# A mixture-of-experts trunk layer: fewer filler matmuls at the start, some in the last pair's waits, and a tail scattered by halves

## The reference

```
h_lat = modulate(rmsnorm(x, g_mix), mod[0], mod[1])     # and h_ctx from ctx
y_lat = token_mixer(h_lat, h_ctx, w_in, ...)
x = x + mod[2] * y_lat
f = modulate(rmsnorm(x, g_ffn), mod[3], mod[4])
# 16 experts in 4 groups; each token goes to the best 2 of its best group
for e in range(16):
    he = silu(f @ w_gate[e]) * (f @ w_up[e])
    y = y + combine[:, e:e + 1] * (he @ w_down[e])
x = x + mod[5] * y
return rmsnorm(x, g_final)
```

## Time and profile before

| | us |
|---|---|
| three runs | 739.55, 743.22, 737.66 |
| median | 739.55 |
| profiled execution, its own time | 739.38 |
| its span, first to last instruction | 737.6 |
| TensorE matmul busy | 704.3 (95% of the span) |
| mean granted TensorE clock | 0.986 |

### The profile page before, as it was taken

One profiled execution on the slowest core, in us unless ns is written; L12 is line 12 of the kernel. 1 busy time (PEld: TensorE's weight loads), 2 busy tenths in 40 slices (PEclk: granted clock), 3 DMA queues, 4 the chain that ended last, 5 costly groups with the idle time before them and its releaser, 6 DMA issues.

```text
span 737.6 us, 7936 instructions
## 1 busy us (share of the span) xinstructions
PE 704.3 (95%) x3260; PEld 419.1 (57%) x3260; DVE 286.8 (39%) x492; ACT 112.3 (15%) x197; POOL 165.9 (22%) x119
## 2 busy tenths in 40 slices
PE   9999999999999999999999999998999999998875
PEld 5334586555775467776877788556434443443321
DVE  2558262877220475644243323235302221220224
ACT  4012011111001322221212320012000000000012
POOL 0137679789197000700000000000000000000020
PEclk9999999999999999999999999998999999999988
DMA  8965355651441333323553235982999999999992
GB/s 357 421 269 202 125 223 198 251 199 58 171 171 58 114 115 120 130 93 115 221 235 113 71 131 207 423 334 120 392 418 423 422 421 423 423 421 423 423 417 96
DMA packets 26388, 183.39 MB, mean 249 GB/s; under 512 B 2928, under 2 KB 3312, under 8 KB 10608
## 3 DMA queue, kind: packets, MB, share of 16 engines
q1 hardware_dynamic: 24336, 176.36, 60.0%
q10 hardware_dynamic: 1440, 4.42, 1.5%
q0 software_dynamic: 576, 2.10, 0.7%
HBM read 178.14 MB, written 4.72 MB: 248 GB/s over the span
## 4 chain that ended last, share of the span: by engine, by line
PE 83%; SPq 7%; DMA 4%; DVE 3%; issue 1%; ACT 0%; DVEq 0%
PE bank L731 17%; PE bank L1096 15%; PE bank L735 9%; PE bank L727 7%; SPq L363 7%; PE bank L748 6%; DMA sb<-expert_w 4%; PE bank L754 4%; PE bank L953 3%; PE bank L1071 3%; PE bank L878 2%; PE bank L899 2%; PE bank L780 2%; PE bank L886 2%; PE bank L741 2%
## 5 line engine op out<-in xcount | busy, mean ns | idle before, releaser
L1096 PE MATMUL bank<-sb 128*64 128x512 f32 x768 | 173.2, 608 | 10.0 <-DMA sb<-expert_w 8.9
L731 PE MATMUL bank<-sb 128*128 128x256 f32 x576 | 128.5, 381 | 0.6 <-PE bank L727 0.3
L1096 PEld LDWEIGHTS bank<-sb 128*64 128x64 f32 x768 | 57.0, 140 | 119.5 <-issue 118.5
L731 PEld LDWEIGHTS bank<-sb 128*128 128x128 f32 x576 | 108.1, 190 | 17.8 <-issue 3.8
L525 POOL DMA_INDIRECT sb<-y_rows,slot_rows x4 | 3.9, 979 | 391.6 <-DMA y_rows<-sb 390.7
L485 POOL TENSOR_TENSOR sb<-sb 128x1024 f32<-128x1024 f32 x32 | 66.4, 2076 | 60.2 <-DMA sb<-ada_w 58.0
L735 PE MATMUL bank<-sb 128*128 128x512 f32 x160 | 70.2, 593 | 0.3 <-PE bank L731 0.3
L1282 DVE COPY sb<-bank 128x512 f32<-128x512 f32 x45 | 29.2, 685 | 105.4 <-PE bank L886 67.2
L727 PE MATMUL bank<-sb 128*128 128x512 f32 x128 | 55.8, 593 | 0.3 <-PE bank L953 0.3
L735 PEld LDWEIGHTS bank<-sb 128*128 128x128 f32 x160 | 29.8, 190 | 35.3 <-issue 35.3
L1613 DVE TENSOR_TENSOR sb<-sb,bank 128x512 f32<-128x512 f32 x8 | 5.5, 689 | 110.8 <-PE bank L1096 110.8
(11 more groups left out here) (237 smaller groups left out, 661.3 us busy)
## 6 DMA issues: line engine op xcount, KB each, us to landing
sb<-expert_w SPq DMA_DIRECT2D x96, 1024.0 KB, 22.1
sb<-front_w SPq DMA_DIRECT2D x19, 2048.0 KB, 8.1
sb<-ada_w SPq DMA_DIRECT2D x32, 512.0 KB, 3.6
sb<-ada_mix SPq DMA_DIRECT2D x4, 2048.0 KB, 19.5
y_rows<-sb ACTq DMA_DIRECT2D x7, 512.0 KB, 7.8
sb<-xcT SPq DMA_DIRECT2D x4, 512.0 KB, 6.3
sb<-front_w SPq DMA_DIRECT2D x4, 512.0 KB, 20.2
sb<-na_bias SPq DMA_DIRECT2D x1, 1536.0 KB, 12.5
```

Source lines behind the costliest of these rows:

```text
L731: ins = pe.matmul(ps[:, c * L:(c + 1) * L], lhs(w, k, (2 * i + c) * P), hT[:, k, 0:L], start=(k == 0), stop=(k == KD - 1))
L1096: ins = pe.matmul(bank[e * CAP:(e + 1) * CAP, :], lhsT[:, k, e * CAP:(e + 1) * CAP], slot[pair_[e]][:, o + k * 512:o + (k + 1) * 512], sta ...
```

## The change

Five edits, in the order of the diff:

- `WARM[0]` goes from 12 to 7: five matmuls of zeros fewer ahead of the row sums.
- `stay_warm(n)` runs n matmuls of 128x512 on constants into bank 1, which nobody reads. One stands ahead of each half of the last pair's `up` (in `two_experts`, for `m == 3 * LAST + 1`), two stand ahead of the first half of its `down`. All stand before the wait for the weights.
- For the last pair TensorE scatters each half directly after its half of `down`: down 0, scatter 0, down 1, scatter 1.
- DVE's order becomes: three of the four gathered blocks, `experts_out` of half 0, the fourth block, `scattered` of half 0, `scaled_tokens`, `experts_out` of half 1, `scattered` of half 1.
- The two loops at the end become one: reciprocal and scaling of token block 0, then of block 1.

```diff
--- before.py
+++ after.py
@@ -81,7 +81,7 @@
 FILLS = [f for g in FRONT if g[:3] != "out" for f in group_fills(g)]
 FILLS += [(f"out{i}", t, "dve") for t in range(NT) for i in range(2)]
 PBANKS = 3
-WARM = (12, 4, 1, 3)
+WARM = (7, 4, 1, 3)
 BANK_OF = [7 if f[:2] == ("ff", 3) else n % PBANKS for n, f in enumerate(FILLS)]
 ROW_GROUPS = (4, 5, 10, 11)
 POOLED = (6, 7, 8, 9, 4, 5, 10, 11)
@@ -1085,10 +1085,17 @@
                 for s in RING[r]:
                     pe.wait_ge(w_in_[s], slot_value(s) + 16 * (5 - LAST) + n * 16)
 
+            def stay_warm(n):
+
+                for _ in range(n):
+                    pe.matmul(banks[1][:, :], ident, small[:, 0:512], start=True, stop=True)
+
             def two_experts(bank, pair_, parts, lhsT, o=0, m=None, n=None):
 
                 for k in range(parts):
                     if m is not None and k % 4 == 0:
+                        if m == 3 * LAST + 1:
+                            stay_warm(1)
                         take_half(m, k // 4)
                     if n is not None and k % 4 == 0:
                         pe.wait_ge(h_out, 2 * n + (k // 4 + 1))
@@ -1134,10 +1141,10 @@
                     ins = pe.transpose(banks[7][:, t * P:(t + 1) * P], SW_now[:, t, :], ident)
                 ins.then_inc(turn_ready, 1)
 
-            def scatter(n):
+            def scatter(n, halves=range(2)):
 
                 pe.wait_ge(cutT_ready, n - (LAST - 1))
-                for i in range(2):
+                for i in halves:
                     pe.wait_ge(y_out, 2 * n + (i + 1))
                     for t in range(NT):
                         pe.matmul(banks[(0, 1, 7, 2)[2 * i + t]][:, :], ST_now[:, t, :], y_sb[:, i * 512:(i + 1) * 512],
@@ -1155,9 +1162,12 @@
                 if n < LAST:
                     gather(n + 1, S_now[(n + 1) % 2], (1,))
                 for i in range(2):
+                    if n == LAST and i == 0:
+                        stay_warm(2)
                     take_half(3 * n + 2, i)
                     down(n, RING[(3 * n + 2) % 5], (i,))
-            scatter(LAST)
+                    if n == LAST:
+                        scatter(n, (i,))
             n_pass = pe.value_load(passes[0:1, 0:1], min_val=1, max_val=MAXPASS)
             with pe.If(n_pass > 1):
                 with pe.Fori(1, n_pass) as p:
@@ -1622,26 +1632,26 @@
                 for t in range(NT):
                     ins = dve.tensor_tensor(xg[:, t, :], x_nat[:, t, 0:512], g_last[:, 0:512], ALU.mult)
 
-            def scattered(n):
-                for i in range(2):
+            def scattered(n, halves=range(2)):
+                for i in halves:
                     for t in range(NT):
                         dve.wait_ge(scat_ready, 4 * (n - LAST) + (2 * i + t + 1))
                         y = x_nat[:, t, 512 * i:512 * i + 512]
                         ins = dve.tensor_tensor(y, y, banks[(0, 1, 7, 2)[2 * i + t]][:, :], ALU.add)
                         ins.then_inc(scat_out, 1)
 
-            def experts_out(n):
+            def experts_out(n, halves=range(2)):
 
                 if isinstance(n, int):
                     dve.wait_ge(y_stored, 16 * n)
-                for i in range(2):
+                for i in halves:
                     dve.wait_ge(down_ready, 2 * n + (i + 1))
                     cols = slice(512 * i, 512 * i + 512)
                     dve.tensor_tensor(y_sb[:, cols], banks[4 + i][:, :], row5[:, cols], ALU.mult).then_inc(y_out, 1)
 
-            def gathered_back():
-
-                for q in range(2 * NT):
+            def gathered_back(rows):
+
+                for q in rows:
                     dve.wait_ge(y_in[q], 16)
                     if q >= NT:
                         dve.drain()
@@ -1671,12 +1681,15 @@
             n_pass = dve.value_load(passes[0:1, 0:1], min_val=1, max_val=MAXPASS)
             gated(LAST)
             turned_out(LAST)
-            gathered_back()
-            experts_out(LAST)
-            scattered(LAST)
+            gathered_back(range(2 * NT - 1))
+            experts_out(LAST, (0,))
+            gathered_back((2 * NT - 1,))
+            scattered(LAST, (0,))
             dve.wait_ge(glast_in, 16)
             dve.wait_ge(scat_out, NT)
             scaled_tokens()
+            experts_out(LAST, (1,))
+            scattered(LAST, (1,))
             with dve.If(n_pass > 1):
                 with dve.Fori(1, n_pass) as p:
                     dve.drain()
@@ -1701,7 +1714,6 @@
             for t in range(NT):
                 dve.wait_ge(fin_root, t + 1)
                 dve.reciprocal(stat[:, 2 + t:3 + t], stat[:, 2 + t:3 + t]).then_inc(fin_rec, 1)
-            for t in range(NT):
                 dve.wait_ge(fin_rec, t + 1)
                 dve.scalar_tensor_tensor(out=normed[:, t, 512:1024], in0=x_nat[:, t, 512:1024], scalar=stat[:, 2 + t:3 + t],
                                          in1=g_last[:, 512:1024], op0=ALU.mult, op1=ALU.mult).then_inc(fin_by["dve"], 1)
```

## The result

| | us |
|---|---|
| kernel before, median of 6 (lowest, highest) | 739.15 (737.66, 743.22) |
| changed kernel, median of 6 (lowest, highest) | 733.27 (732.99, 734.46) |
| ratio | 0.9907, 95% interval 0.988 to 0.9934 |
| profiled execution: own time, span | 733.21, 731.4 |

The ratio stands as recorded; the quotient of the two medians is 0.992. The changed kernel is faster by 0.93%, just under 1%; 735.6 had been forecast, 0.53%. The measured time lies inside the range, but the gain is larger than the sum by more than the measurement leaves open. In the two profiled executions it is 739.38 - 733.21 = 6.17 us, against a sum of 3.97.

The account below looks back on a forecast made before the run. TensorE was taken as the bound, its start passing through the weight stream to the end. 739.38 - 2.15 - 0.92 - 0.9 = 735.4 us for the profiled execution, 0.17 below its median, so 735.6; range 732.5 to 739.0.

Parts of the forecast that it names:

- The bound: Whole kernel: TensorE frees the weight stream's slots, so a microsecond saved at the start moves the stream's end by one.
- The start is hidden: Rival at the start: second gain fails and a modulation block holds TensorE back; 737.4 us, chance 0.13.
- Part 1, five fillers: Start, ahead of the row sums: five fewer warm-up matmuls, at full clock, gain 2.15 us; lower bound 1.2.
- the 0.4 of slack: Start: row sums end at 13.9, so ACT's preparation of the root, ending at 13.52, is in time by 0.4 us.
- The slow rival: Rival at the start: a gap keeps the row sums at half clock, 5.0 us lost; 743.7 us, chance 0.07.
- Part 1, the second gain: First projection: four modulations finish before GpSimd's first big multiply, removing TensorE's wait; gain 0.92 us, bounds 0 and 0.92.
- Part 2, fillers in the last pair: Last pair's up and down waits: fillers keep the clock up; down half 0 takes 3.65 instead of 5.35 us.
- no effect at the end: Last pair: fillers alone are worth nothing, since down's last half waits for weights landing at 722.3 and already takes 3.65.
- Part 3, the tail: From down's last half to the end: scatter by halves and merged final loops gain 0.9 us; bounds 0.3 and 1.3.
- the new wait: Tail: half 0's scatter delays down's last half by 0.36 us; then DVE, not TensorE, starts the last experts_out at 726.8.
- the last wait eats the tail: Rival in the tail: third gathered block lands 2 us later, delaying down's last half; 737.5 us, chance 0.14.
- The clock at the routing: Rival at 504.5 to 511.3 us: the half-clock stretch falls less low, 3.4 us gained; 732.2 us, chance 0.12.

Follow-up runs that it names:

- e1: Kernel before with seven instead of twelve matmuls of zeros at the start, nothing else of the change; median 736.44 us, ratio 0.994.
- e7: Kernel before with twenty-four instead of twelve matmuls of zeros at the start; median 744.0 us, ratio 1.0057.
- e4: Kernel before with one added wait: GpSimd's first big multiply waits until VectorE has modulated all eight blocks; median 739.46 us, ratio 0.997.
- e9: Kernel before, unchanged, run again for a second profile; median 738.98 us.
- e2: Changed kernel with twelve instead of seven matmuls of zeros at the start again; median 736.75 us, ratio 0.9968.
- e10: Kernel before, unchanged, run again for a third profile; median 743.07 us.
- e6: Changed kernel with three instead of seven matmuls of zeros at the start; median 736.13 us.
- e3: Changed kernel without the four filler matmuls in the last pair (both stay_warm calls removed); median 736.2 us, ratio 0.9947.
- e5: Kernel before with the four filler matmuls in the last pair's waits and nothing else; median 741.47 us, ratio 1.0026.
- e8: Changed kernel with six instead of four filler matmuls on TensorE while VectorE works out the routing; median 731.94 us, ratio 0.9899.
- e12: Changed kernel with six routing fillers, the four final stores reordered and the last issued by ScalarE; median 731.21 us, ratio 0.9886.
- e11: Kernel before with fourteen instead of twelve matmuls of zeros at the start; median 741.76 us.

## Why the prediction was right and wrong

**The bound.** Right. The start passes to the end through the weight stream in full: -3.08 at 56 us and -3.08 at 719 (e1), +4.52 and +4.57 (e7). "The start is hidden" is refuted. In single profiles the middle and the routing can hide it (e4, e9).

**Part 1, five fillers.** Forecast 2.15; measured 1.89 (e1) and 2.62 (after). The step from 2.15 to either is the time at which the clock rises, which differs by execution: behind twelve fillers the sums start at 9.03 in before, at 8.59 in e2 and at 9.65 in e10. Also, ScalarE takes over as the limit at 13.5 us, as the 0.4 of slack had it, so fewer fillers than seven bring no more (e6, 13.32). `ada_mix` held nothing up. The slow rival does not occur: even three fillers leave the sums at full clock.

**Part 1, the second gain.** The mechanism was right and the place too; the size was not. This is the step that failed for the kernel's times: "gain 0.92. The bounds are 0 and 0.92". I took one profile's outcome of a race as the largest there is. In that profile it was 1.18 (root to p1 43.30 against 42.12; I left out a second, shorter break in the x16), and in the one profiled execution of the upper group, which holds over a third of them, it is 4.4 with what the clock adds. A price that depends on 0.07 us between two starts, 48.75 and 48.82 (48.77 and 48.88 in e9, where it is nothing), had to be bounded by the worse order, and the first sign was in the table: three runs at 737.66, 739.55 and 743.22. I read these as noise of 1.5 us, where they were two groups.

**Part 2, fillers in the last pair.** Right in what they do to half 0 of `down` (3.65), and in that they can gain only with part 3. Their worth there is 1.4 (e3), close to the delay of 1.3 that I had ahead of the last half; the distance between my bounds was 0.6 all the same (0.9 against 0.3), since I let VectorE's queue hide 0.7 of that delay. It hid nothing: from the last half to the end e3 takes 13.62, as after. What I had as "no effect at the end" by themselves is a loss of 1.7 (e5). The trace of before could not tell me: that its last half ran in 3.65 hung on a wait of 1.22, and I did not ask what a faster half 0 makes of that wait.

**Part 3, the tail.** Forecast 0.9, measured 1.53 (e2, e3, after, to 0.01). Two terms were mis-sized. The first is the drain behind the gathered blocks: I took the 0.52 of idle ahead of L1640 for it, and it stands at two places of my sum. After, the next operation starts 0.07 behind a gathered block (718.71 to 718.78). What the 0.52 was stays open. Without it the scatter of half 0 is done by 717.81, and the 0.36 of delay that I had for the last half shrinks to under 0.1; VectorE is free at 721.46, when TensorE ends its half at 721.45, so the new wait never comes about. The addition ends 7.28 behind the start of the last half instead of 8.01: 0.73 against my 0.33. The second is the stretch from there to the end, 6.33 instead of 7.14: 0.80 against 0.57. The rival "the last wait eats the tail" did not occur in after, where the third gathered block was done at 713.88, 1.0 ahead of half 0 of `down` (714.91). In small it did occur: in e2, e6, e8 and e12 that block was done 0.2 to 0.4 behind half 0, and the last half started up to 0.3 later against its weights than in after (e8, 0.41 behind their landing).

There is a part of the tail's worth that no difference of these two profiles shows: in e10 and e11 the last half ran at half clock in the old order (16.7 from there to the end). With the scatter in the gap, none of the six profiles of the new order did. From the landing of the last weights to the end after takes 13.75 where I had 14.4, and before 15.28.

**The clock at the routing.** I had it as a rival of 3.4 us with 0.12. It gave 1.18 of the 6.17 (7.96 against 6.78). It is luck, not the change: before shows 7.96, 6.78 and 5.15 in three executions, and the kernels with four fillers at the routing and the new order of the tail 6.78, 5.15, 7.81 and 8.24. The two profiles together read: 2.62 + 1.18 - 0.21 (between 59 and 504) + 1.18 - 0.13 (between the first expert matmul and the last half) + 1.53 = 6.17.

So of 2.2 us that the sum lacks, 0.47 is when the clock rose, 0.26 the wait for VectorE, 1.18 the routing and 0.63 the tail, less 0.34 given back between. In these two executions the terms that failed are thus the tail, put at 0.9 where it measured 1.53, and the routing, which the sum put at nothing and which gave 1.18; the first is the change's, the second and the 0.47 are luck. That the medians differ by near the same number, 5.88, is in part chance: before has no one time. Against the middle of its lower group (738.04, of 43 executions) after is 4.8 faster, against that of the upper (742.83, of 34) 9.6. For e1, the start alone, the two distances are 1.6 and 6.4, and my 3.07 for the start stands between them.

## What to carry to other kernels

When the times of a kernel stand in two groups, profile one of each before costing a change: the difference can be a race of a tenth of a microsecond whose price is whole microseconds, and removing it can be the larger part of a gain. Filler that speeds up work off the path lengthens the next wait, and the clock can then fall ahead of the work that is on it; fill the last wait first, with real work if there is some. A saving ahead of a saturated load stream counted in full here, since the stream's start hung on it (e1, e7), and a saving on work that waits for the running stream counted not at all (e5).

## What the hardware showed that I had not expected

- A VectorE addition of 128x8 elements took 1.91 us beside a GpSimd multiply of 1.90 that had started 0.01 us before it; alone it takes 0.17. The Trainium skill, page "GPSIMD Engine Reference", section "8. Key points", names two SBUF inputs as one of the two kinds of VectorE instruction that contend. This addition reads two, and the trace agrees. It is not slowed, it waits until the multiply is over (50.88 and 50.86). e11 shows it again: GpSimd's multiply from 48.79 to 50.68, the addition from 49.93 to 50.70.

```profile
49.93 0.77 DVE L1228 TENSOR_TENSOR sb<-sb 128x8 f32<-128x8 f32 x1
```

- The four slow modulations do the same. In the first profile they end at 50.85, 52.20, 54.17 and 55.51, each 0.14 to 0.15 us behind the end of a GpSimd instruction (50.71, 52.05, 54.02, 55.37); alone one takes 0.41.
- TensorE ran at full speed after three fillers (2.93 us) and 1.92 us of idling (e6: 7.13 for x16, after's 7.03). The profile gives a granted clock of 1.00 from 1.3 us on in before, after and e6; that the first fillers run at half speed stands only in their durations (634 and 379 ns).
- In the tail the halves behind waits of 2.27 us and more ran at half clock and those behind 0.43 to 1.52 at full, with two exceptions: e10 held full clock over a wait of 2.34 and e11 over one of 2.39. The length of the wait alone does not decide.
- From the first projection to L1055, code that no edit touched, it takes 445.1 to 445.3 us in seven of these profiles and up to 447.0 in the others (e9); in e2, e5 and e9 most of the difference is the router's small matmuls, over which the granted clock was 0.67, 0.70 and 0.65 on average, where before has 1.00.
